# A hybrid two-layer step on one core: the order of the first unit, the states and the convolution taps rearranged

## The reference

```python
h = _rmsnorm(x, lp['norm_g']) * (1.0 + scale) + shift      # shift, scale, gate = silu(cond) @ w_ada + b_ada
z = h @ lp['w_in']                                          # conv_in, conv_gate, ssm_in, ssm_gate, q, k, v, attn_gate, merge
br_a = (conformer_conv(conv_in) * silu(conv_gate)) @ w_conv_out   # GLU, depthwise conv of 31 taps, LayerNorm, swish
br_b = (s5_bidirectional(ssm_in) ... * silu(ssm_gate)) @ w_ssm_out # 32 groups x 16 channels, complex state of 64, both ways
br_c = (attention(q, k, v) * silu(attn_gate)) @ w_attn_out  # 8 heads, 2 key heads, RMS-normed, rotary on stream 1
mixed = g_a * br_a + g_b * br_b + g_c * br_c                # sigmoid gates from merge
x = x + gate * (mixed @ lp['w_out'])
```

## Time and profile before

| what | us |
|---|---|
| median of 3 runs (lowest, highest) | 738.4 (738.39, 740.62) |
| the profiled execution | 741.45 |
| its span, first to last instruction | 739.4 |
| TensorE busy in the span | 656.6 |
| VectorE busy | 546.4 |
| ScalarE busy | 291.3 |
| GpSimd busy | 35.4 |
| mean granted TensorE clock | 0.962 of 2.4 GHz |

### The profile page before, as it was taken

The page is one execution under the profiler, slowest core; times in us unless marked ns, Lnnn a source line. Parts: engine busy times, 40 slices in busy tenths (PEclk is TensorE's granted clock), DMA queues, the critical chain, the costliest instruction groups (busy, mean ns, idle before and its releaser), DMA issues.

```text
span 739.4 us, 9579 instructions
## 1 busy us (share of the span) xinstructions
PE 656.6 (89%) x3573; PEld 473.0 (64%) x3573; DVE 546.4 (74%) x1024; ACT 291.3 (39%) x454; POOL 35.4 (5%) x49
## 2 busy tenths in 40 slices
PE   3669679999898999987898797999898999989997
PEld 1357574653744688775787686665485568867885
DVE  3873769994757988988767444899778699897564
ACT  2454322211535454442544642311254345434541
POOL 2100010102000000010000001001200000000000
PEclk9979789999999999998999998999999999999999
DMA  8973623862675365544433347281254236655531
GB/s 283 355 204 97 204 71 118 281 225 57 208 230 173 100 218 165 176 132 124 144 122 105 113 150 274 81 293 54 55 195 121 81 95 194 189 153 151 192 121 57
DMA packets 67305, 117.65 MB, mean 159 GB/s; under 512 B 11052, under 2 KB 15484, under 8 KB 67260
## 3 DMA queue, kind: packets, MB, share of 16 engines
q1 hardware_dynamic: 66980, 116.94, 49.8%
q10 hardware_dynamic: 280, 0.11, 0.1%
HBM read 112.51 MB, written 1.38 MB: 154 GB/s over the span
## 4 chain that ended last, share of the span: by engine, by line
PE 71%; DVE 20%; issue 3%; ACT 3%; SPq 1%; DMA 0%; POOL 0%; ACTq 0%; POOLq 0%; DVEq 0%
PE proj L798 20%; PE proj L826 11%; PE proj L827 11%; PE proj L828 11%; DVE cvacc L1570 4%; PE side L813 3%; DVE raw_split L1463 3%; PE side L951 3%; PE side L965 2%; PE side L1044 2%; PE long L768 2%; PE side L994 2%; DVE tA L1463 1%; DVE tB L1463 1%; PE side L1042 1%
## 5 line engine op out<-in xcount | busy, mean ns | idle before, releaser
L798 PE MATMUL proj<-raw,hT 128*128 128x512 f32 (+1 forms) x320 | 132.0, 558 | 0.0
L1570 DVE SCALAR_TENSOR_TENSOR cvacc<-cvpad,taps,cvacc 128x256 f32<-128x256 f32 x240 | 99.2, 478 | 0.3
L798 PEld LDWEIGHTS proj<-raw,hT 128*128 128x128 f32 x320 | 58.2, 190 | 58.8 <-issue 57.0
L1179 ACT ACTIVATE wide_split<-raw 128x1024 fp32r<-128x1024 f32 x56 | 58.6, 1059 | 58.0 <-PE proj L828 53.2
L1463 DVE TENSOR_TENSOR raw_split<-raw,wide_split 128x1024 fp32r<-128x1024 f32 x56 | 67.6, 1220 | 18.6 <-ACT wide_split L1179 17.6
L827 PE MATMUL proj<-raw_split,H_split 128*128 128x512 f32 x192 | 76.6, 399 | 0.0
L826 PE MATMUL proj<-wide_split,H_split 128*128 128x512 f32 x144 | 59.4, 412 | 12.8 <-DVE raw_split L1463 12.5
L828 PE MATMUL proj<-wide_split,H_split 128*128 128x512 f32 x144 | 58.0, 403 | 0.0
L1463 DVE TENSOR_TENSOR raw_split<-raw,utok_split 128x1024 fp32r<-128x1024 f32 x28 | 34.2, 1221 | 12.6 <-ACT utok_split L1179 12.5
L1179 ACT ACTIVATE utok_split<-raw 128x1024 fp32r<-128x1024 f32 x28 | 29.6, 1058 | 35.1 <-PE proj L828 35.1
L827 PEld LDWEIGHTS proj<-raw_split,H_split 128*128 128x128 f32 x192 | 37.2, 194 | 7.3
(11 more groups left out here) (251 smaller groups left out, 1336.9 us busy)
## 6 DMA issues: line engine op xcount, KB each, us to landing
raw<-in_w_in SPq DMA_DIRECT2D x104, 512.0 KB, 4.2
raw<-in_w_ada SPq DMA_DIRECT2D x48, 512.0 KB, 5.1
raw<-in_w_out SPq DMA_DIRECT2D x16, 512.0 KB, 3.8
raw<-in_w_ssm_glu SPq DMA_DIRECT2D x8, 512.0 KB, 8.2
raw<-in_w_ssm_out SPq DMA_DIRECT2D x8, 512.0 KB, 4.1
raw<-in_w_attn_out SPq DMA_DIRECT2D x8, 512.0 KB, 3.7
raw<-in_w_conv_out SPq DMA_DIRECT2D x8, 512.0 KB, 3.7
raw<-in_w_in SPq DMA_DIRECT2D x8, 256.0 KB, 3.7
```

Of the source, the lines that this page charges most:

```text
L798: m = T.matmul(proj.bank((l, u, s))[:, 0:n], lhs[:, s, kt, :], w[:, i, :], start=(kt == 0), stop=last)
L1179: S.activation(piece_room[m], piece_raw(m), ACT.Copy).then_inc(piece_hi, 1)
L1570: m = V.scalar_tensor_tensor(acc, src, taps[:, t, j:j + 1], acc, ALU.mult, ALU.add)
```

## The change

It touches many places of the list, and some forms of instructions.

- Opening: `tabB` moves from between hT and `early` to behind unit cg. Unit cg of layer 0 goes by passes: the products of the lower four blocks of both streams come after modulation slabs 0 to 3, then slabs 4 to 7, the second half of hT, and the upper four blocks.
- States of layer 0: `cT` and the C loads move ahead of unit ssm, `preE 0` behind unit ca, `pre 1` writes to a buffer of its own in H (`first_pre`), and `bbar` moves behind `cp`. In layer 1 `bbar` moves ahead of unit ca.
- S: a product writes contiguous runs of 64 in PSUM; the evictions read contiguously and write H with a stride of one chunk.
- Taps: 16 (layer 0) or 8 (layer 1) ahead of Y; attention takes 40 + 22 or 30 + 22 in place of 25 + 20; the two merge parts 12 each.
- The modulation transposes move behind Y, and `qkT` of stream 1 ahead of the attention of stream 0.
- Merge of layer 0: `pre` of layer 1 comes later, and its operations alternate with low parts of the slabs.
- Edge: two of the four state evictions come ahead of the squares; the transposes of stream 0 are laid into the last output unit; the last `out_and_add` of layer 0 moves into layer 1's list.

```diff
+TAPS_IN_ZONE = (16, 8)
+TAPS_IN_ATT = (((8, 8, 8, 8, 8), (7, 4, 4, 7, 0)), ((6, 6, 6, 6, 6), (7, 4, 4, 7, 0)))
-    begin = [("unit", "cg"), ("tabC",), ("bT", 0), ("unit", "ssm"), ("cT", 0), ("pre", 0, 0), ("preE", 0, 0),
-             ("chunks", "ca", 4), ("pre", 0, 1), ("unit", "ca"), ("taps", 0), ("pack",), ("preE", 0, 1)]
+    begin = [("unit", "cg"), ("tabB",), ("tabC",), ("bT", 0), ("cT", 0), ("unit", "ssm"), ("pre", 0, 0),
+             ("chunks", "ca", 4), ("pre", 0, 1), ("unit", "ca"), ("taps", 0), ("preE", 0, 0), ("pack",), ("preE", 0, 1)]
     if l:
-        begin = [("hT", 0, 0), ("hT", 1, 0), ("early", 0, 0), ("sq", l, 1), ("early", 1, 0), ("xn", l, 1),
+        begin = [("hT", 0, 0), ("hT", 1, 0), ("early", 0, 0), ("wx", l - 1, 1), ("early", 1, 0), ("sq", l, 1), ("xn", l, 1),
...
-                 ("unit", "ca"), ("pack",)]
+                 ("bbar", l), ("unit", "ca"), ("pack",)]
+    turn = [] if l else [("bbar", l)]
     return (begin
-            + [("bbar", l), ("bz", 0), ("UT",), ("S",), ("cp",), ("convT", 0), ("convT", 1), ("unit", "q"), ("unit", "kv"),
+            + [("UT",), ("S",), ("cp",)] + turn + [("bz", 0), ("convT", 0), ("convT", 1), ("unit", "q"), ("unit", "kv"),
...
-            + [("scan", 0, NCHUNK), ("qkn",), ("adaT", l, 2)] + nxt("adaT", n, 0)
-            + [("conv", 4, None), ("Y",), ("qkT", 0), ("att", 0)] + nxt("adaE", n, 1)
-            + [("geT",), ("qkT", 1), ("att", 1), ("unit", "glub"), ("unit", "glua"), ("split", 0), ("split", 1)]
+            + [("scan", 0, NCHUNK), ("qkn",), ("conv", TAPS_IN_ZONE[l], None), ("Y",), ("adaT", l, 2)] + nxt("adaT", n, 0)
+            + [("qkT", 0), ("qkT", 1), ("att", 0)] + nxt("adaE", n, 1)
+            + [("geT",), ("att", 1), ("unit", "glub"), ("unit", "glua"), ("split", 0), ("split", 1)]
...
-            + nxt("taps", n) + [("cback", 0), ("cback", 1), ("comb", "C", 1)] + nxt("pre", n, 0)
-            + [("brT", "A", 0), ("brT", "A", 1), ("comb", "A", 0)] + nxt("preE", n, 0) + nxt("pre", n, 1)
-            + [("comb", "A", 1), ("wout", 0), ("wout", 1), ("wx", 0)] + nxt("sq", n, 0) + nxt("preE", n, 1)
-            + nxt("xn", n, 0) + [("wx", 1)])
+            + nxt("taps", n) + [("cback", 0), ("cback", 1), ("comb", "C", 1)]
+            + [("brT", "A", 0), ("brT", "A", 1)] + nxt("pre", n, 0) + [("comb", "A", 0)] + nxt("preE", n, 0)
+            + nxt("pre", n, 1) + [("comb", "A", 1), ("wout", 0), ("wout", 1), ("wx", l, 0)] + nxt("preE", n, 1)
+            + nxt("sq", n, 0) + nxt("preF", n, 1) + (nxt("xn", n, 0) or [("wx", l, 1)]))
...
-                            ("tabS",), ("hT", 0, 0), ("hT", 0, 1), ("tabB",), ("early", 0, 0), ("early", 0, 1),
-                            ("ada", 0, 1, 0, DT), ("adaE", 0, 1), ("adaT", 0, 1), ("hT", 1, 0), ("hT", 1, 1),
-                            ("early", 1, 0), ("chunks", "cg", 1), ("early", 1, 1))]
+                            ("tabS",), ("hT", 0, 0), ("hT", 0, 1), ("early", 0, 0), ("early", 0, 1),
+                            ("ada", 0, 1, 0, 4), ("chunks", "cg", 2), ("pass", "cg", 0, 0), ("pass", "cg", 1, 0),
+                            ("ada", 0, 1, 4, DT), ("adaE", 0, 1), ("adaT", 0, 1), ("hT", 1, 0), ("hT", 1, 1),
+                            ("early", 1, 0), ("early", 1, 1), ("pass", "cg", 0, 1), ("pass", "cg", 1, 1))]
...
+        first_pre = H[:, :, :].rearrange("p a b -> p (a b)")[:, 0:2048].rearrange("p (r g j c) -> p r g j c", r=2, g=16, j=L)
+        pre_of = lambda ll, half: first_pre if (ll, half) == (0, 1) else pre
...
+            def tokens_t(l, h, s):
+                pe.wait_ge(xn_second if h else xn_first, ls(l, s))
+                key = ("hT", l, h, s)
+                side.claim(pe, key)
+                for i in range(4):
+                    d = 4 * h + i
+                    m = transpose(side.bank(key)[:, P * i:P * i + P], xn[:, s, P * d:P * d + P])
+                m.then_inc(side.full, 1)
...
-                        out = side.bank(key)[:, :].rearrange("p (k g a r s) -> p g r a s k", k=NCHUNK, g=2, a=2, r=2)
+                        out = side.bank(key)[:, :].rearrange("p (g a r q) -> p g r a q", g=2, a=2, r=2)
...
+                                    if s == 1 and kt == 5 and l + 1 < DEPTH:
+                                        for h in range(2):
+                                            tokens_t(l + 1, h, 0)
...
-                    high_parts(ahead(l, "cg"))
+                    high_parts(ahead(l, "cg", 4))
...
-                        S.activation(H[0:64, 1:NCHUNK + 1, 16 * i:16 * i + 16],
-                                     side.bank(key)[0:64, :].rearrange("p (k x) -> p k x", k=NCHUNK),
+                        dst = H[0:64, 1:NCHUNK + 1, 16 * i:16 * i + 16].rearrange("p k x -> p x k")
+                        S.activation(dst, side.bank(key)[0:64, :].rearrange("p (x k) -> p x k", k=NCHUNK),
                                      ACT.Copy).then_inc(side.freed(key), 1)
...
-                        V.tensor_copy(H[64:128, 1:NCHUNK + 1, 16 * i:16 * i + 16][:, ::-1, :],
-                                      side.bank(key)[64:128, :].rearrange("p (k x) -> p k x", k=NCHUNK)
+                        dst = H[64:128, 1:NCHUNK + 1, 16 * i:16 * i + 16][:, ::-1, :].rearrange("p k x -> p x k")
+                        V.tensor_copy(dst, side.bank(key)[64:128, :].rearrange("p (x k) -> p x k", k=NCHUNK)
...
+                    upto = lambda i: low_parts(piece_at[(l, f"meA{half}", 0)] + i) if ll else None
...
+                        upto(3 * r + 1)
                         needs("pre")
                         makes("first", tt_(t1, lam[0], bb[r]))
+                        upto(3 * r + 2)
                         makes("second", tt_(t2, lam[1], bb[1 - r]))
+                        upto(3 * r + 3)
...
-                        else:
-                            for _ in range(5):
-                                conv_tap(*taps_left.pop(0))
+                        for _ in range(TAPS_IN_ATT[l][s][p]):
+                            conv_tap(*taps_left.pop(0))
```

More of the change, by code:

```diff
@@ L103, in by_pass @@
 def by_pass(l, u):
-    return u == "cg" and l > 0
+    return u == "cg"
 def slab_keys(l, stage):
@@ L116, in slab_keys @@
     if stage[0] == "pass":
-        return [(l, stage[1], kp) for kp in range(DT // KT_SLAB)] if stage[2:] == (0, 0) else []
+        if l:
+            return [(l, stage[1], kp) for kp in range(DT // KT_SLAB)] if stage[2:] == (0, 0) else []
+        return [(l, stage[1], 2 * stage[3] + i) for i in range(2)] if stage[2] == 0 else []
     return [key for u, nk, _ in units_of(stage) for kp in range(nk // KT_SLAB)
@@ L843, in states_in @@
                             m = transpose(side.bank(key)[:, P * i:P * i + P],
-                                          pre[:, r, g:g + 2, :, :].rearrange("p g j c -> p (g j c)"))
+                                          pre_of(ll, half)[:, r, g:g + 2, :, :].rearrange("p g j c -> p (g j c)"))
                         m.then_inc(side.full, 1)
@@ L913, in _ @@
                     h, s = stg[1:]
-                    pe.wait_ge(xn_second if h else xn_first, ls(l, s))
-                    key = ("hT", l, h, s)
-                    side.claim(pe, key)
-                    for i in range(4):
-                        d = 4 * h + i
-                        m = transpose(side.bank(key)[:, P * i:P * i + P], xn[:, s, P * d:P * d + P])
-                    m.then_inc(side.full, 1)
+                    if l == 0 or s:
+                        tokens_t(l, h, s)
                 elif k == "UT":
@@ L950, in _ @@
                             for r in range(2):
-                                m = T.matmul(out[:, gg, r, :, :, :], E[:, r, gp, :],
-                                             Uz[:, 2 * gp:2 * gp + 2, :].rearrange("p a (s k) -> p a s k", s=NS),
+                                m = T.matmul(out[:, gg, r, :, :], E[:, r, gp, :], Uz[:, 2 * gp:2 * gp + 2, :],
                                              start=True, stop=True)
@@ L1236, in _ @@
                                  cT[:, :, :, :].rearrange("p r g c -> p r (g c)"), ACT.Copy).then_inc(cp_done, 1)
-                elif k == "preE":
+                elif k in ("preE", "preF"):
                     ll, half = stg[1], stg[2]
-                    for r in range(2):
+                    for r in ((0,) if stg == ("preE", l + 1, 1) else (1,) if k == "preF" else range(2)):
                         for q in range(2):
@@ L1728, in _ @@
                 elif k == "unit" and stg[1] in ("cg", "ssm"):
-                    low_parts(ahead(l, stg[1]))
+                    low_parts(ahead(l, stg[1], 4 if stg[1] == "cg" else 2))
                 elif k == "UT":
@@ L1763, in _ @@
                         side.drained(dve, ("bT", ll, i))
-                    side.filled(dve, ("E", ll, 3) if half else ("cT", ll, 1))
+                    if half == 0:
+                        side.filled(dve, ("cT", ll, 1))
+                    elif ll:
+                        side.filled(dve, ("E", ll, 3))
```

(16 more changed lines are left out.)

12 lines of the change are left out of this document (8 added, 4 removed).

## The result

The changed kernel takes **719.46 us** (median of 4 runs, 717.9 to 721.32) against 738.82 (738.39 to 740.62) for the kernel before: a ratio of **0.9734**, 95% interval 0.9702 to 0.9767. Measured once more it was 0.9718 (0.9699 to 0.9738). That lies in the range of 698 to 724, above the forecast's own 701 to 714 and among the times of rival 1 (714 to 728).

A forecast was written before the change was run, and what follows sets the result against it. TensorE's product stream plus its waits, mostly for VectorE, was taken to bound the kernel; stage gains and losses summed to 31.7 us off the 738.4 median, giving 707 (range 698 to 724, own range 701 to 714, 58%).

The forecast's parts named there:

- rival 1: Merge gains turn into waits for VectorE as states and parts hold each other: 714 to 728 us, chance 22%.
- Start: Layer 0's first unit in halves, tables behind it: first product at 34.1, end near 58, 1.5 us lost.
- To S: First unit to S, layer 0: two waits go, VectorE's chain becomes the long one; S begins 8.4 us earlier.
- 16 transposes, their evictions of 0.6 and UT, about 5.5: Last step before S in layer 0, after VectorE's states: about 5.5 us, in a chain of 37 us.
- The 2.2 us: Gain inside S, per layer: 8.6 us with the last eviction, against 10.28 + 0.6 with three tiles at half clock.
- S to Y: Layer 0, S's end to Y: VectorE 0.4 us later, TensorE waits some 4 us ahead of Y instead of 3.12.
- Attention: Layer 0: more taps per step make stream 0 end later; 3 us lost (1 to 5), clock's fall included.
- 0.6 for a part of a fall of the clock: Part of layer 0's attention loss: 0.6 us added to a net 2.4 lost, making 3.
- the forecast of 0.4: Attention of layer 1, with six taps a step: 0.4 us lost.
- Merge and edge: Layer 0's merge gains 3.2 us, then 9.8 in A0 and A1; the second pass starts 3.3 earlier at the edge.
- the 1.5 us left ahead of A0: Merge, A0: with state operations and slab parts interleaved, 1.5 us of the 5.09 us wait stay.
- C0 of layer 1: Merge of layer 1: 7 taps fewer at C0 gain 2.8 us (0 to 4).

The follow-up runs named there:

- e1: Changed kernel with layer 0's first unit undivided again, tables still behind it: 713.31 us, ratio 0.9608 to the kernel before.
- e4: Changed kernel with ScalarE's copy for UT ahead of layer 0's state evictions and the taps' transposition behind both: 717.67 us, ratio 0.9687 to the kernel before.
- e2: Changed kernel with S in its old form, strided PSUM writes and evictions in runs of 16: 719.59 us, ratio 0.9716 to the kernel before.
- second profile: Changed kernel measured and profiled again with nothing changed: 720.68 us, ratio 0.9718 to the kernel before.
- c3: Changed kernel with the edits of e1, e3 and e4, plus 12 layer 0 taps moved to C0, 8 from ahead of Y: 695.08 us, ratio 0.9388.
- e3: Changed kernel with the same number of attention taps, none in stream 0's last two steps: 712.82 us, ratio 0.9627 to the kernel before.

## Why the prediction was right, and where 11 us went

**Start.** Right in its steps: first product 34.21 (forecast 34.1), the 24 products until 41.4 (41.6), second half at 49.84 (near 51), end at 57.7 (near 58), half clock twice. Two errors cancel in the end: the four slabs took 1.9 us, not 3.0, and the second 24 products 7.9, not 7. What the forecast did not do is compare the halves with their own alternative: undivided, the unit would have ended at 52.5 (e1).

**To S.** The VectorE chain was right: the states are done at 88.1, forecast 89.4. The step that failed is "16 transposes, their evictions of 0.6 and UT, about 5.5": it took 8.4. ScalarE's copy of 1.90 us stood between the evictions and was not in the count, and the transposition of the taps held a bank for 2.48 us until VectorE's copy at 89.25. With both out of the way it takes 4.7 (89.49 to 94.15, e4); how much of it is either one was not separated.

**S.** ScalarE's eviction was right (1.05 forecast, 1.05), VectorE's 0.695 was not (1.04). The Trainium skill (Advanced Engine Details and Errata, Memory Cachelines) says that accesses that change their 16-byte line each time pay. VectorE's write agrees with it, 1.04 us against 0.69 in runs of 16, where the row of its read the earlier trace rows had not. S did not get longer by it (e2). The same section's warning on broken runs in PSUM shows nowhere here: 7.38 us with and without. The 2.2 us were those of the clock, and come where it holds: 8.2 us from S to q in the second profile, forecast 8.6.

**S to Y.** 16 taps (0.73 and 5.62 us, from 174.80) ended at 181.07, and VectorE's first copy of H after them: a wait of 5.45 where 4 was forecast. c3 shows that half of it goes with 8 taps.

**Attention.** The waits were right (4 to 5 forecast, 3.86, of which 1.9 are new), their consequence was not: "0.6 for a part of a fall of the clock" measured 2.6 us (2.04 + 5.28 against 1.10 + 3.60), and Y itself ran 0.8 longer, at 0.54 from 182 to 188 behind its longer wait. In layer 1 the forecast of 0.4 left the fall out; it cost the other 2. The waits there, 1.70 and 0.95, are together no longer than the 1.31 and 1.82 of before, but the clock fell behind the first of them: it is 0.57 from 549 to 557 us and was 1.00 from 570 to 578, and the scores and eight products take 2.04 and 4.60 us, where they took 1.10 and 3.60. This term is the largest error, 4.5 us in both layers, and e3 settles it.

**Merge and edge.** 10.3 for 9.8, 2.6 for 3.2, 4.3 for 3.3; the 1.5 us left ahead of A0 measured 1.58. In C0 of layer 1 the profiled execution gained 1.2 instead of 2.8, having a stretch at 0.50 from 580 to 583; in the second profile the same stage takes 60.49 us against 63.31: 2.8. There the merge of layer 0 paid instead, 66.66 us to C1 where the first profile has 65.16.

So where a wait was removed its clock was counted as gained, and where a wait was added its clock was left out or put at a quarter. That asymmetry, with the copy on ScalarE and the bank of the taps missed ahead of S, is most of the 10.7 us. That the time stayed inside the range is in part luck: the range reached to 724 to take in rival 1, and the time lies there by another cause.

## What to carry to other kernels

Price a new wait on TensorE like a removed one: its length and the half-speed stretch that may follow, which cost 2.6 to 2.7 us at S and at the scores of layer 0 here. Work laid into an engine's gaps is free only if nothing that frees a shared buffer stands behind it: 8 taps of 0.41 us cost little in the first steps of attention and held the accumulator in the last two. And compare a reordering with its nearest alternative, not only with the kernel before: here the halves of the first unit lost 6 us, hidden in a gain of 19.

## What the runs showed of the hardware

The granted clock at one and the same place can differ between executions of one kernel: S of layer 0 at 0.50 behind waits of 2.48, 1.61 and 0.98 us, and at 1.00 behind 2.52, 1.04 and 1.01, where the fall came earlier, at the transposes. Nor does the length of the waits alone say whether it falls: in layer 1, between the streams of attention, it stayed at 1.00 behind 1.31 and 1.82 us in the kernel before and fell to 0.50 behind 1.70 in the changed one. And a VectorE copy from PSUM that writes 512 elements per partition at a wide stride takes 1.04 us, against 0.69 in runs of 16, about the same as ScalarE's 1.05 against 0.59.
